# State mixer's jobs ahead of the attention's at each point, and its within-chunk products in column halves

## The chip, the cores and the metric

One Trainium2 chip, one of its cores. The metric is the device time of one execution in microseconds. Five engines work side by side, each through its own list in order: TensorE (PE; its weight loads are shown as PEld), VectorE (DVE), ScalarE (ACT), GpSimd (POOL) and SyncE (SP), which issues most transfers. Semaphores order them against each other.

## What is computed

One layer of a diffusion backbone over 512 latent tokens (width 1024) and 256 context tokens: a norm with modulation, one input projection, four token mixers side by side, a gated merge, an output projection, and a mixture of experts. Two of the mixers matter here. Cut to what matters:

```python
def _window_attention(q, k, v, k_ctx, v_ctx, sink):      # 8 heads, 4 blocks of 128 queries
    s_loc = einsum("bqkgd,bjkd->bkgqj", qn, kn) * scale  # window of 3 blocks, masked
    s_ctx = einsum("bqkgd,bckd->bkgqc", qn, k_ctx) * scale
    probs = softmax(concatenate([s_loc, s_ctx, sink_col], -1))
    return p_loc @ vn + p_ctx @ v_ctx

def _ssd(x, dt, a, bm, cm, init, with_output):           # 8 heads, chunks of 128, forward and backward
    a_cs = cumsum(dt * a); xd = x * dt[..., None]
    chunk_states = einsum("bcqhn,bcqhp->bchpn", bc * decay_to_end[..., None], xd)
    final, prev = scan(step, init, (chunk_states, chunk_decay))
    lmat = exp(where(tri, a_cs[i] - a_cs[j], -inf))
    scores = einsum("bcihn,bcjhn->bcijh", cc, bc) * lmat
    y_diag = einsum("bcijh,bcjhp->bcihp", scores, xd)    # the within-chunk products
    y_off = einsum("bcihn,bchpn->bcihp", cc, prev) * exp(a_cs)[..., None]

def _merge(h, branches, w_gate, b_gate, w_branch, w_o):
    gates = sigmoid(h @ w_gate + b_gate)
    return sum(gates * einsum("blnw,nwd->blnd", branches, w_branch)) @ w_o
```

## The kernel before

The order of work is written out by hand. `timeline()` (lines 70 to 149) returns one list of steps, and every engine's program walks through that same list, each issuing its own instructions of a step. So a step's place in the list is its place in the queue of PE, DVE, ACT and POOL at once, and what an engine waits for in one step holds up all steps behind it on that engine. `bank_plan` (line 196) gives each step its bank of PSUM; `claim` (line 578) makes PE wait until the former user of the bank was read.

The stretch of interest is the merge. For each of the four branches in `MIX_ORDER` (3 short convolution, 2 Fourier, 0 attention, 1 state mixer) and each of 8 column tiles d there is a step `gate` (24 products of 128x512) and a step `proj` (12 of them). Behind each of them `side()` (line 125) is called twice; each call is a point, counted by `point`. On odd points it gives out the next step of the attention, on even points the next entry of the state mixer's list `ssm`.

The attention's steps work on a pair of heads or on one: `S` makes scores (DVE scales, masks and takes the maximum, lines 1798 to 1821; ACT takes the exponentials), `T` transposes the probabilities on PE (line 1045; on DVE a `T` step of odd number normalises two later heads, line 1822; ACT copies the result to PT), `O` multiplies with the values (line 1054; DVE copies the result to attT, line 1830). A block of queries with five key blocks takes the fifth one's scores in the bank that `O` uses.

The state mixer's steps, for direction d, chunk c and group g:

- `st`: the state of a chunk. POOL makes xdd (line 2190), PE multiplies (line 976), DVE combines it with the former state (lines 1831 to 1847: tmpS, then prevS). All ten use one bank.
- `G`: products of C and B for a chunk, masked on DVE to Gm (line 1848).
- `seg`: the decay matrix of a chunk and group. POOL fetches the decay rows with a broadcasting transfer to Am once the former E is made (line 2202), subtracts and clips in 4 instructions for each direction (line 2206), and for g = 0 also makes xd (line 2211), for which it waits for `y` of the former chunk. ACT takes the exponential to E (line 1415) once the former `y` no longer reads E. DVE multiplies E by Gm (line 1861).
- `yoff`: products with the former states (line 995), read by DVE with a factor (line 1862).
- `y`: the within-chunk products (line 1008), 4 heads by 2 directions of 128x128 weights (E) over 64 columns (xd), accumulated; DVE adds all parts and multiplies by the gate z (line 1869).
- `ynorm`, `ytr`: the norm and the transposes at the end.

Each product of 32-bit operands appears in the trace as two passes.

Two more names. Each weight tile of the stream is split in two parts that together keep its precision: ring_hi on ACT, ring_lo on DVE, also at steps of the list (`split_at`). At the first `proj` of each branch the branch itself is split in bhi (ACT) and blo (DVE), lines 1426 to 1434 and 1893 to 1898. The experts' first weights are fetched by SP once the last merge is done (line 652).

The list of the state mixer before, for one chunk c, has six entries, that is three pairs of gate and proj:

```python
scans += [[G(c,0), G(c,1), seg(c,0,0), seg(c,0,1)], [], [yoff(c,0), yoff(c,1)],
          [y(c,0)], [seg(c,1,0), seg(c,1,1)], [y(c,1)]]
```

Of the kernel before, what the change touches and what calls it, by code (L numbers as in the profile page):

```python
# [26 lines left out]
P = 128  # L27
# [5 lines left out]
HD = 64  # L33
# [11 lines left out]
HALF = BLK // 2  # L45
# [24 lines left out]
def timeline():  # L70

    t = [("mr", 0), ("ssq",), ("mr", 2), ("mod", 0), ("xa", 0), ("mr", 1), ("xa", 1), ("mr", 3), ("modb",), ("csq",), ("xbc", 0)]
    t += [("v", c) for c in range(NCH)]
    t += [("ssqc",), ("xbc", 1), ("fu", 0), ("xbcc", 0), ("vc",), ("xbcc", 1), ("dt",)]
    macc = 0

    def tile(*jobs):


        nonlocal t, macc  # L80
        t += [*jobs, ("macc", macc)]
        if macc > 4 and macc % 4 == 1:
            t += [("mod", macc // 4)]
        macc += 1

    for m in range(2, 6):
        tile(("xbc", m), ("xbcc", m))
    tile(("k",), ("kc",))
    for m in range(1, 4):
        tile(*([("rope", 0)] if m == 2 else []), ("fu", m), *([("rot", 0)] if m == 1 else []))  # L90
    t += [("dec",)]
    for m in range(4):
        tile(*([("rope", m - 1)] if m > 1 else []), ("q", m), *([("rot", m)] if m else [("decr",)]))
    for m in range(4):
        tile(*([("rope", 3)] if m == 0 else []), ("cg", m), *([("rot", 4)] if m == 0 else []))
        tile(*([("rope", 4)] if m == 0 else []), ("sx", m))
        if m < 3:
            tile()
        tile(("bg", m))
    for i in range(4):  # L100
        tile(("zk", i))
    t += [("macc", 31)] + [("z", c) for c in range(NCH)]
    t += [("xtr", c) for c in (4, 5, 0, 1, 2, 3)] + [("btr", 0), ("btr", 1), ("mod", 8)]

    att_step = 0

    def attention():

        nonlocal att_step
        h, att_step = att_step, att_step + 1  # L110
        even = h % 2 == 0
        return ([("O", h // 2 - 2)] * (even and h >= 4) + [("T", h - 2)] * (2 <= h < 34) + [("S", h // 2)] * (even and h < 32))

    t += attention() + [("V", 0), ("V", 1), ("F", 0), ("V", 2), ("F", 1), ("V", 3)] + attention()
    t += [("F", 2), ("F", 3)] + attention() + attention()

    ssm = [[("st", d, k)] for k in range(5) for d in range(2)]
    scans = [[], [], []]
    for c in range(NCH):
        scans += [[("G", c, 0), ("G", c, 1), ("seg", c, 0, 0), ("seg", c, 0, 1)], [], [("yoff", c, 0), ("yoff", c, 1)],  # L120
                  [("y", c, 0)], [("seg", c, 1, 0), ("seg", c, 1, 1)], [("y", c, 1)]]
    scans += [[("ynorm",)], []] + [[("ytr", c), ("ytr", c + 1)] for c in (0, 2)]
    point = 0

    def side():

        nonlocal point
        point += 1
        if point % 2 == 1 and att_step < 35:
            return attention()  # L130
        if ssm and point % 2 == 0:
            return ssm.pop(0)
        return []

    for i, n in enumerate(MIX_ORDER):
        if i == 1:
            ssm += scans
        if i == 3:
            t += [x for jobs in ssm for x in jobs]
            ssm = []  # L140
        for d in range(8):
            t += [("gate", n, d)] + side() + side() + [("proj", n, d)] + side() + side()
    for d in range(8):
        if d == KD - 1:
            t += [("rtk", 5), ("rtf",)]
        t += [("wo", d)] + ([("sw",)] if d == 4 else []) + ([("rtk", d - 2)] if 1 < d < KD - 1 else [])
    t += [("rtk", 6), ("ssq2",), ("rtk", 7), ("rt",)] + [("h2tr", c) for c in range(NCH)] + [("g2",), ("cnt",), ("pick", 0), ("bexp",), ("pick", 1),
                                                                   ("up0",), ("tab",)]
    return t
# [158 lines left out]
def build(nc, xT, ctxT, adaw, stream, consts, cossin, dft, cols, rows, wv, wrt, umap, wa, wb, w2, h2d, ybuf, csd, gfin, out):  # L308
# [29 lines left out]
    E = at("E", 65536, [P, 2, S])  # L338
# [32 lines left out]
    xd = at("xd", 173248, [P, 2, S])  # L371
    H = at("H", 177344, [P, KD, S])
    CT = at("CT", 193728, [P, C_N])
    o = 193728 + C_N * 4
# [92 lines left out]
    def bk(b, n=1):  # L467

        return psum[:, b:b + n, :].rearrange("p b n -> p (b n)")
# [234 lines left out]
    def _(pe):  # L704
        def mm(out, lhsT, rhs, start, stop):
            return nc.tensor.matmul(out, lhsT, rhs, start=start, stop=stop)  # L706
# [112 lines left out]
        for s in steps:  # L819
            k0 = s[0]  # L820
            if k0 in ("ssq", "ssqc"):
                b = claim(pe, s)
                pe.wait_ge(sum_ready, 1 if k0 == "ssq" else 2)
                if k0 == "ssq":
                    ins = mm(bk(b), one_t[:, :], sq[:, 0, :], True, True)
                else:
                    for i in range(2):
                        ins = mm(bk(b)[:, 0:SC], one_t[:, :], sq[:, KD, i * SC:i * SC + SC], i == 0, i == 1)
                ins.then_inc(full[b], 1)
            elif k0 == "mod" and s[1]:  # L830

                b = claim(pe, s)
                pe.wait_ge(macc_ready, 4 * s[1])
                for j in range(4):
                    ins = mm(bk(b)[:, 2 * j:2 * j + 2], macc[s[1] % 2][:, j * P:j * P + P], CT[:, C_ONE:C_ONE + 2], True, True)
                ins.then_inc(full[b], 1)
            elif k0 == "mr":

                b = claim(pe, s)
# [11 lines left out]
                for k in range(KD):  # L851
                    q = k % 4 * 32
                    ins = mm(bk(b)[q:q + 32, :], silp[:, k, :], ada[u][:, k * S:k * S + S], k < 4, k >= 4)
# [30 lines left out]
            elif s == ("xbc", 0):  # L884
# [8 lines left out]
                for k in range(4, KD):  # L893
                    ins = lo_block(k)
# [11 lines left out]
            elif k0 == "vc":  # L906
                b = claim(pe, s)
                pe.wait_ge(h_ready, 2 * KD)
                for i in range(NCC):
                    for k in range(KD):  # L910
                        ins = mm(bk(b)[:, i * VD:i * VD + VD], hcx[:, k, i * P:i * P + P], WV[:, k, :], k == 0, k == KD - 1)
                ins.then_inc(full[b], 1)
            elif k0 == "zk":
# [3 lines left out]
                for c in range(NCH):  # L917
                    b = claim(pe, ("z", c)) if s[1] == 0 else plan[("z", c)][0]
                    for kk in range(2):
                        k = 2 * s[1] + kk  # L920
                        ins = three(bk(b), Hhi[:, k, c * P:c * P + P], Hlo[:, k, c * P:c * P + P], hi[:, kk * S:kk * S + S],
                                    lo[:, kk * S:kk * S + S], k == 0, k == KD - 1)
# [6 lines left out]
            elif k0 == "dec":  # L929
                b = claim(pe, s)  # L930
                pe.wait_ge(dta_ready, 1)
                sums = bk(b)[:, 0:288].rearrange("p (c n) -> p c n", n=48)
                for col, (m, r0, r1) in zip((0, 8, 16, 24, 32), ((C_LE, 0, 8), (C_GE, 8, 16), (C_GT, 0, 8),
                                                                 (C_LT, 8, 16), (C_ONE, 0, 16))):
                    ins = mm(sums[:, :, col:col + r1 - r0], CT[:, m:m + P], dta[:, :, r0:r1], True, True)
                ins.then_inc(full[b], 1)
            elif k0 == "decr":
                b = claim(pe, s)
                pe.wait_ge(csr_ready, 1)
                nc.tensor.transpose(bk(b)[0:NCH * 16, 0:P], csr[:, :, :].rearrange("p c n -> p (c n)"), ID).then_inc(full[b], 1)  # L940
            elif k0 == "xtr":
                b = claim(pe, s)
                pe.wait_ge(xbc_ready, 6)
                o = chunk_cols(s[1])
                for m in range(4):
                    ins = nc.tensor.transpose(bk(b)[:, m * P:m * P + P], xbcT[:, m, o:o + P], ID)
                ins.then_inc(full[b], 1)
            elif k0 == "btr":
                b = claim(pe, s)
                for i in range(3):  # L950
                    o = chunk_cols(3 * s[1] + i)
                    ins = nc.tensor.transpose(bk(b)[:, i * P:i * P + P], xbcT[:, 4, o:o + P], ID)
                ins.then_inc(full[b], 1)
            elif k0 == "V":
                b = claim(pe, s)
# [6 lines left out]
                for c in range(NCH):  # L962
                    ins = mm(bk(b, 2)[:, c * 256:c * 256 + 256], uT[:, ft, c * P:c * P + P],
                             CT[:, C_BD:C_BD + 256], True, True)
                ins.then_inc(full[b], 1)
            elif k0 == "F":
                b = claim(pe, s)
# [8 lines left out]
            elif k0 == "st":  # L976
                d, k = s[1:]
                b = claim(pe, s)
# [29 lines left out]
            elif k0 == "y":  # L1008
# [3 lines left out]
                pe.wait_ge(xd_ready, 2 * (c + 1))  # L1012
                for h in range(4):
                    for d in range(2):
                        ins = mm(bk(b)[:, h * HD:h * HD + HD], E[:, d, h * P:h * P + P],
                                 xd[:, d, (g * 4 + h) * HD:(g * 4 + h) * HD + HD], d == 0, d == 1)
                ins.then_inc(full[b], 1)
            elif k0 == "ytr":
                b = claim(pe, s)
# [1405 lines left out]
```

## Time and profile before

| what | value |
|---|---|
| time, median of 3 runs | 1158.52 us (1158.37 to 1160.19) |
| the profiled execution's own time | 1160.84 us |
| its span, first to last instruction | 1159.0 us |
| PE busy | 1094.2 us, 94% of the span |
| DVE, ACT, POOL busy | 562.2, 317.3, 178.7 us |
| mean granted clock of TensorE | 0.986 of full speed |
| chain that ended last | PE 71%, DMA 14%, DVE 8%, ACT 3% |

The profile is of one execution. Times in it count from the first instruction. A group of instructions is told by its line, its engine and what it writes and reads; line 706 is the helper through which all products of PE go, line 1547 that of most of DVE's, line 1244 that of ACT's. Behind an instruction or group stands the time for which its engine sat idle before it, and what ended that. The merge lies between 280 and 647 us.

### The profile page before, as it was taken

Reading aid. Unit: us, or ns where it says so; the run is one execution under the profiler, and the core shown is the slowest. Engines: PE = TensorE matmul, PEld = TensorE weight load, DVE = VectorE, ACT = ScalarE, POOL = GpSimd, SP = SyncE. Lnnn points to the kernel's source line nnn. Section 1 sums busy time; section 2 is a strip of 40 time slices with the busy share of each in tenths; the row PEclk is TensorE's granted clock in tenths of the full one; section 3 lists DMA queues with packets and bytes.
Section 4 is the critical chain, followed back from the end, with each engine's and each line's share of the span. In section 5 each row is a group of like instructions: output and inputs, shape, how many; then the busy total and the mean of one; then the engine's idle time right before and its main releaser. Section 6 shows DMA issues by size and latency. Waiting matters only on the chain.

```text
span 1159.0 us, 16301 instructions
## 1 busy us (share of the span) xinstructions
PE 1094.2 (94%) x5691; PEld 701.2 (61%) x5691; DVE 562.2 (49%) x1011; ACT 317.3 (27%) x539; POOL 178.7 (15%) x255
## 2 busy tenths in 40 slices
PE   6999999989999999999999998999999899978985
PEld 4788888878667777878888777333333233322333
DVE  5776787744676778757564547221112111111214
ACT  4543322244344554333433242100000000000003
POOL 0000010000110223256000100122212112211220
PEclk9999999999999999999999998999999999999998
DMA  9523855720111122214122488999999999999975
GB/s 373 202 95 117 299 170 202 254 92 19 56 55 56 73 74 74 90 74 146 56 109 93 178 369 331 406 379 424 424 423 425 425 424 426 426 427 425 426 313 224
DMA packets 41982, 279.68 MB, mean 241 GB/s; under 512 B 7803, under 2 KB 8187, under 8 KB 30017
## 3 DMA queue, kind: packets, MB, share of 16 engines
q1 hardware_dynamic: 34496, 265.07, 56.9%
q0 software_dynamic: 7424, 13.80, 3.5%
q8 instruction: 38, 0.62, 0.2%
q14 instruction: 24, 0.19, 0.0%
HBM read 274.23 MB, written 13.40 MB: 248 GB/s over the span
## 4 chain that ended last, share of the span: by engine, by line
PE 71%; DMA 14%; DVE 8%; ACT 3%; issue 2%; POOL 1%; SPq 0%; DVEq 0%; ACTq 0%; POOLq 0%
PE psum L706 68%; DMA ering<-in_wb 8%; DMA ering<-in_wa 2%; DMA ada<-in_adaw 2%; DVE ring_lo L1547 1%; PE psum L722 1%; DVE amx L1818 1%; ACT ring_hi L1244 1%; DVE sc L1807 1%; PE psum L1052 1%; DMA xr<-token_rows,tabt 1%; PE psum L746 1%; DMA Hx<-in_xT 1%; POOL Am L2206 1%; PE psum L1136 0%
## 5 line engine op out<-in xcount | busy, mean ns | idle before, releaser
L706 PE MATMUL psum<-ering,xs 128*64 128x512 f32 x1056 | 240.2, 606 | 17.4 <-DMA ering<-in_wb 9.4
L706 PE MATMUL psum<-Hhi,ring_hi 128*128 128x512 f32 x472 | 188.0, 398 | 0.1
L706 PE MATMUL psum<-Hlo,ring_hi 128*128 128x512 f32 x472 | 185.3, 393 | 0.2 <-DVE Hlo L1547 0.2
L706 PE MATMUL psum<-Hhi,ring_lo 128*128 128x512 f32 x472 | 183.1, 390 | 0.0
L706 PEld LDWEIGHTS psum<-ering,xs 128*64 128x64 f32 x1056 | 74.0, 139 | 162.1 <-issue 137.5
L1547 DVE TENSOR_TENSOR ring_lo<-ring,ring_hi 128x1024 fp32r<-128x1024 f32 x87 | 107.9, 1240 | 107.8 <-ACT ring_hi L1244 106.7
L1547 DVE TENSOR_TENSOR sg<-sg,psum 128x256 f32<-128x256 f32 x66 | 27.8, 421 | 238.3 <-ACT sg L1244 237.2
L706 PE MATMUL psum<-ering,at 128*64 128x512 f32 x528 | 119.5, 597 | 2.8 <-ACT at L1244 1.6
L1244 ACT ACTIVATE ring_hi<-ring 128x1024 fp32r<-128x1024 f32 x87 | 92.2, 1060 | 74.8 <-DMA ring<-in_stream 41.8
L706 PEld LDWEIGHTS psum<-Hhi,ring_hi 128*128 128x128 f32 x472 | 88.7, 188 | 22.7 <-issue 3.2
L706 PEld LDWEIGHTS psum<-Hhi,ring_lo 128*128 128x128 f32 x472 | 88.5, 188 | 19.7
L706 PEld LDWEIGHTS psum<-Hlo,ring_hi 128*128 128x128 f32 x472 | 88.7, 188 | 18.1 <-DVE Hlo L1547 0.5
L1244 ACT ACTIVATE sg<-psum 128x256 f32<-128x256 f32 x33 | 12.7, 384 | 250.4 <-PE psum L706 250.4
L706 PEld LDWEIGHTS psum<-ering,at 128*64 128x64 f32 x528 | 35.9, 136 | 67.1 <-issue 66.4
L1547 DVE TENSOR_TENSOR ysb<-psum,G 128x512 f32<-128x512 f32 x33 | 22.8, 691 | 94.9 <-PE psum L706 80.6
L2206 POOL TENSOR_SCALAR Am<-Am,csr 128x128 f32<-128x128 f32 x64 | 53.7, 852 | 33.9 <-DMA Am<-decay_rows 33.2
L706 PE MATMUL psum<-bhi,ring_hi 128*128 128x512 f32 x128 | 53.2, 416 | 2.4 <-DVE blo L1547 2.4
L706 PE MATMUL psum<-blo,ring_hi 128*128 128x512 f32 x128 | 51.0, 398 | 0.0
L706 PE MATMUL psum<-bhi,ring_lo 128*128 128x512 f32 x128 | 50.9, 398 | 0.0
L1244 ACT ACTIVATE gth<-psum,half 128x512 f32<-128x512 f32 x32 | 22.0, 689 | 102.4 <-PE psum L706 100.0
L1244 ACT ACTIVATE at<-psum 128x256 f32<-128x256 f32 x33 | 12.7, 384 | 124.0 <-PE psum L746 124.0
L2234 POOL DMA_INDIRECT expert_rows<-ysb,idx x33 | 33.7, 1020 | 84.0 <-DVE ysb L1547 83.1
(355 smaller groups left out, 1447.0 us busy)
## 6 DMA issues: line engine op xcount, KB each, us to landing
ering<-in_w SPq DMA_DIRECT2D x28, 2048.0 KB, 21.6
ering<-in_wb SPq DMA_DIRECT2D x28, 2048.0 KB, 27.8
ering<-in_wa SPq DMA_DIRECT2D x28, 2048.0 KB, 22.8
ring<-in_stream SPq DMA_DIRECT2D x87, 512.0 KB, 4.2
ada_ring<-in_stream SPq DMA_DIRECT2D x32, 512.0 KB, 3.6
ada<-in_adaw SPq DMA_DIRECT2D x4, 2048.0 KB, 10.7
Am<-decay_rows POOLq DMA_DIRECT2D x8, 512.0 KB, 4.6
gat<-expert_rows SPq DMA_DIRECT2D x4, 1024.0 KB, 8.1
```

Source lines behind the costliest of these rows:

```text
L706: return nc.tensor.matmul(out, lhsT, rhs, start=start, stop=stop)
L722: ins = nc.tensor.transpose(XT[h][:, q * P:q * P + P], xr[h][:, q * P:q * P + P], ID)
L746: ins = nc.tensor.transpose(AT[h][:, q * P:q * P + P], sg[h][:, q * P:q * P + P], ID)
L1052: ins = nc.tensor.transpose(bk(b, 2)[:, i * P:i * P + P], sc[:, h % 3, i * P:i * P + P], ID)
L1244: return nc.scalar.activation(out, in_, f, **kw)
L1547: return V_.tensor_tensor(out, a, b, op)
L1807: ins = V_.scalar_tensor_tensor(sc[:, h % 3, 0:S], bk(3 + g), HD ** -0.5, CT[:, C_MASK + mo:C_MASK + mo + S], ALU.mult, ALU.add)
L1818: link(V_.tensor_reduce(amx[:, h, 0:1], sc[:, h % 3, 0:W], AX.X, ALU.max))
L2206: G_.tensor_scalar(Am[:, d, h * P:h * P + P], Am[:, d, h * P:h * P + P], csr[:, c, x:x + 1], 0.0, ALU.subtract, ALU.min).then_inc(*t(am_re ...
L2234: G_.indirect_dma_start(out=row_half, in_=rows_[:, :], in_offset=None, out_offset=bass.IndirectOffsetOnAxis(ap=idx[:, 2 + h:3 + h], axis=0 ...
```

## The change

Attention and state mixer change places: the state mixer's steps come on odd points, the attention's on even ones, so at each gate and proj the state mixer's step stands first in the list. In each chunk `seg(c,1)` moves one entry forward, to stand right behind `y(c,0)`; with `seg(c,0)` in the first entry the segments are now three entries apart. `y(c,1)` keeps its entry. And `y`'s products are issued in halves of 64 weight columns, which write to the lower and the upper 64 partitions of the bank.

```diff
@@ timeline
         scans += [[("G", c, 0), ("G", c, 1), ("seg", c, 0, 0), ("seg", c, 0, 1)], [], [("yoff", c, 0), ("yoff", c, 1)],
-                  [("y", c, 0)], [("seg", c, 1, 0), ("seg", c, 1, 1)], [("y", c, 1)]]
+                  [("y", c, 0), ("seg", c, 1, 0), ("seg", c, 1, 1)], [], [("y", c, 1)]]
@@ side
-        if point % 2 == 1 and att_step < 35:
+        if point % 2 == 0 and att_step < 35:
             return attention()
-        if ssm and point % 2 == 0:
+        if ssm and point % 2 == 1:
             return ssm.pop(0)
@@ PE, step y
                 for h in range(4):
                     for d in range(2):
-                        ins = mm(bk(b)[:, h * HD:h * HD + HD], E[:, d, h * P:h * P + P],
-                                 xd[:, d, (g * 4 + h) * HD:(g * 4 + h) * HD + HD], d == 0, d == 1)
+                        for i in range(2):
+                            o = h * P + i * HALF
+                            ins = mm(bk(b)[i * HALF:i * HALF + HALF, h * HD:h * HD + HD], E[:, d, o:o + HALF],
+                                     xd[:, d, (g * 4 + h) * HD:(g * 4 + h) * HD + HD], d == 0, d == 1)
```

## Rows read from the trace of the kernel before

**Rows 1.** Busy time by stretch: window, length, busy and count by engine, clock, DMA share, GB/s

```profile
252.00:645.00 393.00, 379.65 (x2199) 304.32 (x2200) 254.32 (x475) 160.81 (x266) 79.35 (x89) 0.99 0.21 73
...
800.00:1000.00 200.00, 194.84 (x904) 65.90 (x906) 36.09 (x68) 12.58 (x33) 41.65 (x68) 0.99 1.01 425
```

**Rows 2.** Waits of PE, 252 to 660: who for whom, us in total, times, longest

```profile
PE psum L706 <- DVE prevS L1547: 3.9, 4, 1.2
PE psum L706 <- DVE blo L1547: 2.4, 1, 2.4
PE psum L706 <- DVE attT L1830: 2.4, 4, 0.8
PE psum L706 <- DVE yt L1547: 1.7, 2, 1.5
PE psum L706 <- DVE tmpS L1841: 1.6, 1, 1.6
```

**Rows 3.** Timeline of DVE and PE at the second st: start, length, instruction [idle before]

```profile
290.05 0.69 DVE L1807 SCALAR_TENSOR_TENSOR sc<-psum,CT 128x512 f32<-128x512 f32 x1
...
293.44 0.42 DVE L1841 COPY tmpS<-psum 128x256 f32<-128x256 f32 x1
...
293.92 0.65 PE L706 MATMUL psum<-xdd,btm 128*64 128x256 f32 x4 [1.63 <-DVE tmpS L1841]
```

**Rows 4.** Timeline of PE: first product of a gate, and of the proj behind it

```profile
589.01 0.40 PE L706 MATMUL psum<-Hhi,ring_hi 128*128 128x512 f32 x1
...
594.53 0.39 PE L706 MATMUL psum<-bhi,ring_hi 128*128 128x512 f32 x1
```

**Rows 5.** Timeline of DVE, 434 to 442: the reads of yoff

```profile
437.36 0.69 DVE L1547 TENSOR_TENSOR ytmp<-psum,dec 128x512 f32<-128x512 f32 x1
438.09 0.69 DVE L1547 TENSOR_TENSOR yt<-psum,dec 128x512 f32<-128x512 f32 x1
```

**Rows 6.** Timeline of ACT, POOL and DVE, 484 to 512: two segments, then the branch split

```profile
487.20 1.30 ACT L1244 ACTIVATE E<-Am 128x512 f32<-128x512 f32 x2
...
489.03 0.78 POOL L2202 DMA_DIRECT2D Am<-decay_rows  x1 [14.64 <-ACT E L1244]
...
502.43 0.63 ACT L1244 ACTIVATE E<-Am 128x512 f32<-128x512 f32 x1 [4.20 <-POOL Am L2206]
...
505.52 2.50 DVE L1547 TENSOR_TENSOR blo<-attT,bhi 128x512 fp32r<-128x512 f32 x4
```

**Rows 7.** Busy time by stretch: the first proj of the attention branch

```profile
506.35:510.72 4.37, 4.37 (x12) 3.20 (x12) 2.89 (x4) 1.77 (x3) 2.17 (x2) 0.65 0.34 138
```

**Rows 8.** Groups by line, 252 to 660, POOL: busy us, mean ns | idle before

```profile
L2206 POOL TENSOR_SCALAR Am<-Am,csr 128x128 f32<-128x128 f32 x64 | 53.7, 852 | 33.9 <-DMA Am<-decay_rows 33.2
...
L2211 POOL TENSOR_TENSOR xd<-xs,dtv 128x512 f32<-128x512 f32 x8 | 9.7, 1212 | 0.6 <-PE psum L706 0.6
```

**Rows 9.** The page's DMA issues: count, KB each, us to landing

```profile
Am<-decay_rows POOLq DMA_DIRECT2D x8, 512.0 KB, 4.6
```

**Rows 10.** Timeline of PE: products of O, y, the modulation and an expert

```profile
438.84 1.31 PE L706 MATMUL psum<-PT,vt 128*64 128x128 f32 x20 [1.46 <-DVE yt L1547]
...
441.76 2.00 PE L706 MATMUL psum<-xd,E 128*128 128x64 f32 x16
...
252.06 1.05 PE L706 MATMUL psum<-CT,macc 128*128 128x2 f32 x8 [0.64 <-ACT btm L1244]
...
980.04 7.09 PE L706 MATMUL psum<-ering,xs 128*64 128x512 f32 x32
```

**Rows 11.** Groups by line, 252 to 660, PE and PEld: y's products, the two loads

```profile
L706 PE MATMUL psum<-xd,E 128*128 128x64 f32 x128 | 15.5, 274 | 0.0
...
L706 PEld LDWEIGHTS psum<-PT,vt 128*64 128x64 f32 x288 | 15.4, 136 | 7.2 <-issue 5.0 <-DVE yt L1547 1.9 <-DVE Gm L1547 0.4
L706 PEld LDWEIGHTS psum<-xd,E 128*128 128x128 f32 x128 | 15.2, 192 | 0.7 <-issue 0.2
```

**Rows 12.** The tile Am: duration of its instructions, ns least, median, most

```profile
L2206 POOL TENSOR_SCALAR Am<-Am,csr x64: 702/716/1667, 398.3 to 547.3; 128x128 f32<-128x128 f32 x64
```

## The prediction

> **What bounds the kernel now.** The profiled execution took 1160.84 us, 1.84 us more than its span of 1159.0; the median of the three runs is 1158.52. I sum the change against the profiled execution and then set it off from the median, which lies 2.3 us lower. First the table by stretch: in the stretch of the gate and projection products, 252 to 645 us, TensorE (PE) is busy for 379.65 of 393 us, VectorE (DVE) for 254, ScalarE (ACT) for 161 and GpSimd (POOL) for 79 [rows 1]. So PE sets the pace, and two things can be won: its 13 us of idle time, and instructions of its own. The experts behind it run on weight transfers (DMA share 1.01 from 800 to 1000 us [rows 1]), and by the code the first of these waits for the last merge. So what the stretch loses in length, the end should lose too.
>
> Second, the waits of PE [rows 2]: 3.9 + 1.6 us behind the state combinations on DVE (prevS, tmpS), 1.7 behind `yoff` and `y` work (yt), 2.4 behind the split of the attention branch (blo), 2.4 behind the copy of attention rows (attT). All are head-of-line waits: DVE works its list in order, and the wanted instruction stands behind attention work.
>
> **Part 1: `st` ahead of the attention.** PE reached the second `st` when its bank was still unread: the read, tmpS at 293.44, stood on DVE behind the two softmax heads that began at 290.05; PE went on at 293.92 after 1.63 us idle [rows 3]. After the change `st` leaves PE and DVE before O, T and S, so its bank is read while PE does attention and a projection (2.8 us, half of the gate's 5.5 [rows 4]). I take all of 3.9 + 1.6 = 5.5 us away (bounds: 3 to 5.5). What is late next: the projection's `st` is read at most 1 us after the projection's own DVE pair, and the next `st` is a whole gate (5.5 us) later. POOL's product for the next `st` waits only for the former `st` on PE, which comes earlier too. On the other side, DVE's copy of O now stands behind `st`, and the fifth key block of S waits for that copy. Three of the four attT waits lie in places without `st` and stay; the one with `st` can grow by the two DVE instructions of a combination less the `st` products that now fill PE: 0.85 us (an estimate, twice the 0.42 of tmpS [rows 3]) less 0.55, so +0.3.
>
> **Part 2: `yoff` and `y` ahead.** At 437 PE waited 1.46 us for yoff's reads, which stood behind two softmax normalisations; the reads take 0.69 each from 437.36 [rows 5]. Placed ahead they end sooner by the two normalisations, more than the wait: the 1.7 us of yt waits go to nothing (bounds 0.3 to 1.7). New waits stand in their place. On PE `y` waits for the masked E and for xd, and O, T and S are now queued behind it; its segment is two or three points back, a gate at least, so I count no wait. On ACT the second segment's exponentials wait for `y`, and the copy of T is queued behind them; the next O needs it a gate later. On DVE `y` and the masking of E (`seg`) stand ahead of O and S: DVE begins S's heads some 3 us later in four places (an estimate). The next transposes of probabilities stand a projection and a gate away, and by my count 1.4 us remain at the tightest (an estimate). I set +1.5 us for new waits over the stretch (bounds 0 to 6): nothing in the trace shows this order, and the remaining slack is nearest to nothing lost.
>
> **Part 3: `seg` three points apart.** Before, the second segment's exponentials (E at 487.20) waited on ACT for their place behind two transposes and a projection, POOL's next transfer waited 14.64 us for them (489.03), and the last exponential began at 502.43 and ended at 503.06; behind it in line stood the copies and splits of which blo, from 505.52, is the one that PE's first projection of the attention branch needs [rows 6]; PE began it at 506.35 [rows 7]. After the change the segment stands right behind `y(c,0)`, which follows the gate: six us earlier. What is late next is `y(1,1)`, for which POOL waits before its product xd. It stands ahead of O now; behind its end PE still has O (1.1), a projection (2.8), two small G (0.4, an estimate) and a gate (5.5), 9.8 us. In that time POOL makes xd (1.2) and four Am of 0.85 [rows 8], ACT an exponential (0.63), and the rest takes 506.35 − 503.06 = 3.3 as before: 8.5. It leaves 1.3 us, so the 2.4 go (bounds 1 to 2.4). With them goes a second loss: right behind this gap the granted clock was 0.65 over 506.35 to 510.72 [rows 7], that is in part at the lower of its two levels, 1.2 GHz, and the projection took 4.37 us instead of 2.8: 1.5 us. Sum 3.9.
>
> A transfer of decay rows, a POOL queue entry, moves with the segment; 4.6 us to landing [rows 9] at a DMA share of 0.21 [rows 1] is covered. Moved past it on that queue is nothing but `st` products, long done.
>
> **Part 4: within-chunk products in column halves.** Eight `y`, each 16 passes of 128 weight columns over 64 moving columns. From the timeline: (2.00 − 0.27) / 15 = 0.115 us a pass, and 8 passes over only 2 moving columns take (1.05 − 0.25) / 7 = 0.114 [rows 10] (the last pass taken off, 0.27 [rows 11]; 0.25 for the narrow one is an estimate). So a pass costs what loading 128 columns costs, whatever moves. The change makes 32 passes of 64 columns, in two column groups. Loading 64 columns takes 192 − 136 = 0.056 us less than 128 [rows 11], that is half. And two column groups work at once: O's 20 passes of this shape over 128 columns take 1.31 us, (1.31 − 0.27) / 9.5 = 0.109 for a pair (0.27 for the last pass [rows 11]; half a pair more for the first load), and 32 over 512 take 7.09, at most 0.443 a pair [rows 10]. Four times the columns, four times the time: no floor shows down to 0.109, and the loading hides. At 64 columns a pair should take 0.056, and 16 pairs with a first load and a change of array shape 0.9 + 0.16 = 1.05 us against 1.8. I take 0.75 × 8 = 6.0 us (bounds: 0, if 0.109 is the least for a pair, to 7). No semaphore is added.
>
> The Trainium skill speaks against this part. "TensorE: Matmul & The Clock Gate", Part 3, What overlaps, says that loading weights overlaps running products only where the row groups differ; column halves use the same rows. By that rule load and product follow each other and the sum would lose the 6 us. The trace disagrees as far as O reaches: its pairs at 0.109 leave no room for a load of 0.056 beside 128 columns [rows 10], and O's groups share their rows.
>
> **Sum.** −5.5 + 0.3 − 1.7 − 3.9 − 6.0 + 1.5 = −15.3 us. Profiled 1160.84 − 15.3 = 1145.5; from the median 1158.52 − 15.3 = **1143.2 us**.
>
> **Rivals.**
> *The halves give nothing* (a pair has a floor at O's 0.109: 16 × 0.109 + 0.1 = 1.8 us, as now). For it: no row has a shorter pair. Against it: the proportion from 128 to 512 columns. Time 1158.5 − 9.3 = 1149.2. The skill's rule above would give the same.
> *DVE becomes the queue that PE waits for*: with `y` and `seg` ahead of S, the probabilities come late in the chunks that still have attention. DVE is at 65% of the stretch [rows 1], so it needs a bad order, not too much work. If DVE is 3 us later than I count in the four places, and 1.4 of each is slack, PE waits 4 × 1.6 = 6.4 us more: 1143.2 + 6.4 = 1149.6, and with the halves giving nothing 1155.6.
> *The waits only move*: PE meets the same unread banks at the gate's `st`. Then 5.5 us come back: 1148.7. Against it: a gate of 5.5 us stands between.
> *Slower: POOL's decay chain becomes the bound.* Per chunk it has two transfers of 4.6 [rows 9], 16 Am of 0.85, two xd of 1.2 [rows 8], and about 3.5 of issue and exponentials: 28.7 us. PE's chunk without attention is 3 × (5.5 + 2.8) + 1.5 + 2 × 1.05 = 28.5 (estimate), so there is no slack beyond what chunk edges give. If Am rose to the 1.67 us of its slowest one [rows 12], a chunk would take 41.8; chunks 2 and 3 and the wait for the normalisation would cost PE 2 × 13 = 26 us against 15 won, 1169. It decides from a mean Am of about 1.5. For it: Am goes from 0.70 to 1.67 in one trace, so something does stop it. The skill's "GPSIMD Engine Reference", 1. Specifications, names the memory interface shared with VectorE as such a thing. Against it: the mean is 0.85 at the present load, DVE's work is not more, and `y` stands two points behind its segment.
> *It doesn't do what it says*: the instructions are issued in the order of the list, so only the halves could fail this, and that is the first rival.
>
> **How the numbers follow.** Forecast as summed 0.62; halves give nothing 0.17; DVE late, or waits that move, 0.12; POOL chain 0.05; mixtures that end near no change 0.04. What a measurement of this kernel can tell from no change is about 0.2%, 2.3 us. Faster by more 0.87; the same 0.06; slower 0.07 (the chain and half of the mixtures). The range: downwards all bounds at their best, −5.5 − 1.7 − 3.9 − 7 = −18.1, 1140.4, and 1.4 for how the executions differ: 1139. Upwards the halves at 0 and 3 us of waits beyond what I set, 1152.2: 1152.
>
> **What would show it.** In the trace after: no PE waits for tmpS, prevS, yt and blo, and attT waits of 2.4 to 2.7 us; the granted clock at 1.00 at the first projection of the attention branch; `y` at 32 passes of 128*64 within 1.1 us, where 1.8 would show the floor; POOL's wait for E between the segments shorter than 14 us and the Am mean near 0.85. The forecast is wrong if PE's idle time in the stretch is still above 9 us, if new waits for probabilities (T behind DVE's sc) appear, or if the length won in the stretch is lost again between the last merge and the experts.

## The result and the profile after

The changed kernel takes 1152.93 us (median, 1151.3 to 1153.95), the kernel before 1158.52 beside it: a ratio of 0.9946, 95% interval 0.9931 to 0.996. It is faster, by 5.6 us and not by the 15.3 forecast, and 0.9 us above the range. The profiled executions differ by 1160.84 − 1152.93 = 7.9 us. The whole difference lies in the merge. From the first product of its first gate to the first product of the output projection behind it, PE took 647.20 − 279.88 = 367.3 us before:

```profile
279.88 0.47 PE L706 MATMUL psum<-Hhi,ring_hi 128*128 128x512 f32 x1
...
647.20 0.39 PE L706 MATMUL psum<-mhi,ring_hi 128*128 128x512 f32 x1
```

And now:

```profile
279.76 0.48 PE L706 MATMUL psum<-Hhi,ring_hi 128*128 128x512 f32 x1
...
639.26 0.39 PE L706 MATMUL psum<-mhi,ring_hi 128*128 128x512 f32 x1
```

that is 359.5, so −7.8; what comes behind it to the end of the span takes 511.8 us in both. I call this the length of the merge below. It is read from the same two products in each trace, and it leaves out the stretches ahead (278.3 to 280.9 us over all traces) and behind (510.2 to 513.2). But it is the length in one execution of each kernel, with the clock that this execution happened to be granted; the whole times are of 5 to 17 executions.

The waits of PE from 252 to 660 us (who for whom, us in total, times, longest) answer to [rows 2]:

```profile
PE psum L706 <- DVE attT L1832: 4.6, 5, 1.9
PE psum L706 <- DVE Gm L1549: 2.1, 1, 2.1
PE psum L1054 <- DVE sc L1589: 1.4, 1, 1.4
...
PE psum L706 <- DVE tmpS L1843: 0.9, 1, 0.9
...
PE psum L706 <- DVE ring_lo L1549: 0.3, 1, 0.3
PE psum L706 <- DVE blo L1549: 0.2, 1, 0.2
```

yt and prevS are gone, blo and tmpS nearly so. Gm and sc are new, and attT has grown from 2.4 to 4.6. Within the merge PE waited 12.05 us before (the five rows of [rows 2]) and waits 9.45 now. By stretch (window, length, busy and count of PE, PEld, DVE, ACT, POOL, clock, DMA share, GB/s), against [rows 1] and [rows 7]:

```profile
252.00:645.00 393.00, 381.68 (x2357) 303.34 (x2357) 260.35 (x482) 163.93 (x268) 81.37 (x92) 0.99 0.23 77
...
462.00:470.30 8.30, 7.18 (x34) 5.58 (x34) 6.38 (x15) 2.12 (x5) 6.79 (x8) 0.61 0.01 4
501.20:504.20 3.00, 2.98 (x14) 2.18 (x14) 2.96 (x4) 1.67 (x2) 3.00 (x3) 1.00 0.56 175
```

The first projection of the attention branch, at 501, now runs at full clock. But from 462 the granted clock is 0.61, right behind the new waits. What they cost and where they come from is one story on three engines. The timeline (start, length, instruction, [idle before]) of DVE, ACT and PE around 456 us:

```profile
454.39 0.21 DVE L1821 TENSOR_SCALAR amx<-amx,RW 128x1 f32<-128x1 f32 x1
454.70 0.72 ACT L1246 ACTIVATE sc<-sc,amx 128x512 f32<-128x512 f32 x1 [0.69 <-DVE amx L1821]
...
455.73 1.06 ACT L1246 ACTIVATE ring_hi<-ring 128x1024 fp32r<-128x1024 f32 x1
...
456.89 1.23 DVE L1549 TENSOR_TENSOR ring_lo<-ring,ring_hi 128x1024 fp32r<-128x1024 f32 x1 [2.29 <-ACT ring_hi L1246]
...
458.15 0.69 DVE L1907 SCALAR_TENSOR_TENSOR mtmp<-gth,psum 128x512 f32<-128x512 f32 x1
...
459.60 1.01 DVE L1549 TENSOR_TENSOR Gm<-psum,CT 128x128 f32<-128x128 f32 x4
...
460.64 1.42 DVE L1549 TENSOR_TENSOR E<-E,Gm 128x512 f32<-128x512 f32 x2
...
460.66 1.09 PE L706 MATMUL psum<-PT,vt 128*64 128x128 f32 x16 [2.11 <-DVE Gm L1549]
...
462.49 0.49 DVE L1589 TENSOR_SCALAR sc<-sc,amx 128x512 f32<-128x512 f32 x1
...
463.12 1.09 PE L1054 MATMUL psum<-CT,sc 128*128 128x128 f32 x4 [1.36 <-DVE sc L1589]
```

DVE ends the last maximum of S at 454.60. Next in its list is ring_lo, the second half of a weight split for a gate two column tiles on. It needs ring_hi, which on ACT stands behind the exponentials of the same S, and these wait for the maximum that DVE has just made. So DVE stands still for 2.29 us, although mtmp and Gm behind ring_lo could run: what they read is long made. The masking of E could not, as its E comes from ACT, behind the same ring_hi. O finds its bank (the one of G) unread for 2.11 us, T finds its probabilities not normalised for 1.36 (DVE's normalisation, sc at 462.49, comes behind Gm and E), and the clock falls. It is no isolated place. The waits of DVE in the merge up to the last `y`, first of the kernel before, then of the changed one:

```profile
DVE ring_lo L1547 <- ACT ring_hi L1244: 40.7, 22, 5.7
```

```profile
DVE ring_lo L1549 <- ACT ring_hi L1246: 40.7, 20, 6.2
```

That row was in the trace of before, and it is not among the rows that the prediction rests on.

### The profile page after: what moved, and what is told of

The parts are those of the page before. It is cut to its first block, busy times and chain, and to the rows that moved or that the text cites. A ratio compares the mean times of both kernels' runs of the same rounds, so it can differ in the third digit from the quotient of the medians.

```text
span 1151.1 us, 16557 instructions
## 1 busy us (share of the span) xinstructions
PE 1086.0 (94%) x5819; PEld 693.4 (60%) x5819; DVE 563.5 (49%) x1011; ACT 317.2 (28%) x539; POOL 178.4 (16%) x255
## 4 chain that ended last, share of the span: by engine, by line
PE 70%; DMA 15%; DVE 9%; ACT 3%; issue 2%; SPq 0%; DVEq 0%; POOL 0%; ACTq 0%; POOLq 0%
PE psum L706 66%; DMA ering<-in_wb 8%; DMA ering<-in_wa 2%; DMA ada<-in_adaw 2%; DVE ring_lo L1549 2%; PE psum L1054 1%; ACT ring_hi L1246 1%; PE psum L722 1%; DMA xr<-token_rows,tabt 1%; PE psum L746 1%; DVE amx L1820 1%; DMA WV<-in_wv 1%; DVE sc L1809 1%; DMA gat<-expert_rows 0%; ACT gth L1246 0%
## 5 line engine op out<-in xcount | busy, mean ns | idle before, releaser
L706 PE MATMUL psum<-ering,xs 128*64 128x512 f32 x1056 | 237.0, 599 | 19.1 <-DMA ering<-in_wb 10.8
L706 PEld LDWEIGHTS psum<-Hhi,ring_hi 128*128 128x128 f32 x472 | 88.7, 188 | 20.4 <-issue 1.1
```

## The experiments

Two theories of where the missing 9.7 us (15.3 − 5.6, in the medians) went. **Queue**: the change does what the sum says, but DVE's splits that wait for ACT stand in its list between the moved steps, so the time saved on PE is met by new waits of PE for DVE. **Small parts**: one or more terms of the sum (halves, order, segment) are simply worth less than forecast. The second can be seen by doing one part alone, the first by moving the splits. All ratios are to runs of the kernel before on the same chip.

**The halves alone.** Only the hunk of `y` in the diff, with the order of before.

```diff
...
+                        for i in range(2):
+                            o = h * P + i * HALF
+                            ins = mm(bk(b)[i * HALF:i * HALF + HALF, ...], E[:, d, o:o + HALF], ...)
```

> The kernel before with the products of y in column halves and nothing else. If each y falls from 1.7 to 1.8 us to about 1.0 and PE alone sets the pace, eight of them give 5.7 us: 1152.8 from 1158.5. If the freed time is taken back by the waits that are already there (the split of the attention branch behind POOL's decay chain, 2.4 us, would grow), 1155 or more. If both halves of the change were independent, this and the order alone would add up to the whole.

Measured: 1157.36, ratio 0.9979 (0.9968 to 0.9991); length of the merge 362.1. The eight `y` fall as in the changed kernel (8.6 us in all, start to start, for 13.9), but the median shows less than half of it. The reason that the expectation gave for this is not what the trace shows: the wait for blo did not grow (2.1 for 2.4), and PE's waits in the merge are 12.6 us for 12.05. The traced execution was the fastest of its twelve.

**The order alone.** The changed kernel without the hunk of `y`.

```diff
-                        for i in range(2):
...
+                        ins = mm(bk(b)[:, h * HD:h * HD + HD], E[:, d, h * P:h * P + P], ...)
```

> The changed kernel with y at full width: the order and the segments as changed, the column halves undone. If the halves are worth the 5.7 us that the trace shows for y, this is 1158.6, no gain at all from the order, its old waits (8.0 us and a slow projection) replaced by new ones (4.9 us and a slow gate). If the halves only shift waits, it lies near 1153.

Measured: 1153.48, ratio 0.9941 (0.9925 to 0.9957); merge 362.9, that is −4.5 where the order's terms sum to −9.3. The first expectation, 1158.6 and no gain at all, missed by 5 us; the time is that of the other, by which the halves only shift waits. In the whole times the halves on top of this order indeed show nothing clear of the noise (ratios 0.9941 and 0.9946); in the traces they shorten the merge by 3.4, as 2.0 of their 5.3 us turn into waits of PE (7.43 us in the merge here, 9.45 in the changed kernel). Its waits of PE, 252 to 660 us:

```profile
PE psum L706 <- DVE attT L1830: 4.5, 5, 1.9
...
PE psum L1052 <- DVE sc L1587: 1.4, 1, 1.4
...
PE psum L706 <- DVE tmpS L1841: 0.9, 1, 0.9
PE psum L706 <- DVE Gm L1547: 0.5, 1, 0.5
```

So the new waits come with the order (two stretches of low clock too, see the end); with the shorter `y` the one for Gm is 2.1 instead of 0.5.

**State steps ahead only while `st` lasts** (point 32), then as before.

```diff
+        swap = point <= 32
-        if point % 2 == 1 and att_step < 35:
+        if point % 2 == (0 if swap else 1) and att_step < 35:
-        if ssm and point % 2 == 0:
+        if ssm and point % 2 == (1 if swap else 0):
```

> The kernel before with the state steps alone ahead of the attention (the first branch), the scans behind it as before, y at full width. The five waits of 5.5 us should go, 0.9 come at the second of the gate's st, and the wait for the copy of attention rows grow by 1.1: 3.5 us, 1155.0. If the order of st does nothing but move waits, 1158.

Measured: 1153.86, ratio 0.9955 (0.9941 to 0.997); merge 360.4. Of the `st` waits 0.9 is left (tmpS), attT is 3.5, yt stays at 1.7, and blo falls to 1.4 though the segment has not moved. This part alone gives nearly all that the whole change gives, so the rest of it wins and loses about the same.

**The segment alone** moved behind `y(c,0)`, with all else as before.

```diff
-                  [("y", c, 0)], [("seg", c, 1, 0), ("seg", c, 1, 1)], [("y", c, 1)]]
+                  [("y", c, 0), ("seg", c, 1, 0), ("seg", c, 1, 1)], [], [("y", c, 1)]]
```

> The kernel before with the second segment moved to stand right behind y(c,0) and nothing else (attention still ahead, full-width y). Prediction's Part 3: the wait for blo (2.4 us) goes and the projection behind it runs at full clock (1.5 us): 3.9 us below before, 1155. Rival: with y and state behind the attention as before, the chain from the segment to blo is as long as it was and the wait stays: no change from before, 1158.5 to 1159.5.

Measured: 1157.11, ratio 0.9981 (0.997 to 0.9992), between the two expectations; merge 364.0, −3.3. The wait for blo fell from 2.4 to 0.4 and no low clock follows it (timeline of PE):

```profile
504.92 0.47 PE L706 MATMUL psum<-bhi,ring_hi 128*128 128x512 f32 x1 [0.40 <-DVE blo L1547]
```

**Late splits.** The changed kernel; on DVE a ring_lo that is listed at a `proj` is made at the next gate. Nothing is left out, only DVE's order changes.

```diff
+        late = []
...
+            if k0 in ("gate", "wo") or s in split_at and k0 != "proj":
+                for i in late:
+                    split_lo(i)
+                late = []
+            if k0 == "proj":
+                late += split_at.get(s, [])
+            else:
                 for i in split_at.get(s, []):
                     split_lo(i)
```

> The changed kernel; on DVE alone the low part of a weight tile that falls due at a projection (every second one) is made at the next gate instead, ahead of nothing that PE needs within 12 us. Theory: the new waits of PE (0.9 at an st, 1.1 more at the fifth key block, 2.1 at O and 1.4 at T in the second chunk, and the half clock behind them, about 2.5) come from DVE standing idle 2.3 us there for the high part, which on ACT is queued behind the exponentials of the scores that DVE has just made. Then they go and the time falls by 5 to 8 us, to 1145 to 1148. Rival: DVE has simply too much work in those places; then the waits stay and the time is 1152 to 1153.

Measured: 1145.17, ratio 0.9874 (0.9856 to 0.9892); merge 352.4. The waits for Gm, sc and tmpS are gone, and no low clock is left in the merge. What is left of PE's waits there, beside 0.3 and 0.2 for ring_lo and blo:

```profile
PE psum L706 <- DVE attT L1840: 4.0, 5, 1.2
...
PE psum L706 <- ACT PT L1246: 0.4, 1, 0.4
```

DVE goes on standing still for ring_hi, 30.5 us in 12 places instead of 40.7 in 20. So the idle time as such is not what costs; it costs where work that PE wants soon stands behind it.

**All splits late**: those listed at O, `st` and `y` too, to just ahead of the next projection or gate.

```diff
+        late, merging = [], False
...
+            if k0 in ("gate", "proj", "wo"):
+                for i in late:
+                    split_lo(i)
+                late, merging = [], True
+            if merging and k0 not in ("gate", "wo"):
+                late += split_at.get(s, [])
+            else:
                 for i in split_at.get(s, []):
                     split_lo(i)
```

> The changed kernel, with all of DVE's ring_lo splits of the merge that do not belong to the step at hand put behind the work that TensorE waits for: those that stood ahead of a projection are made at the next gate, those that stood ahead of O, st or y are made just before the next projection or gate. Queue theory (DVE stood still for ACT's ring_hi with wanted work behind it): the attT waits (1.24 and three of .54) and the wait of G(2,0) (1.12) go too, 3 to 4 us below the 1145.2 of late_split, so 1141 to 1142, with no wait of TensorE above 0.6 us between 280 and 636 us. Rival (what is left is DVE's and ACT's own pace of work): nothing more is won, 1145.

Measured: 1139.3, ratio 0.9827 (0.9811 to 0.9843), beside 1152.59 for the changed kernel on the same chip; merge 346.9. This beats both kernels, and the expectation by 2 us. PE has no wait in the merge any more, and DVE hardly one for ring_hi; the same place as above, all in its order:

```profile
DVE ring_lo L1549 <- ACT ring_hi L1246: 0.8, 1, 0.8
```

```profile
449.30 0.21 DVE L1829 TENSOR_SCALAR amx<-amx,RW 128x1 f32<-128x1 f32 x1
449.55 0.69 DVE L1915 SCALAR_TENSOR_TENSOR mtmp<-gth,psum 128x512 f32<-128x512 f32 x1
...
450.64 1.06 ACT L1246 ACTIVATE ring_hi<-ring 128x1024 fp32r<-128x1024 f32 x1
451.00 1.01 DVE L1549 TENSOR_TENSOR Gm<-psum,CT 128x128 f32<-128x128 f32 x4
...
454.87 1.09 PE L706 MATMUL psum<-PT,vt 128*64 128x128 f32 x16
...
455.78 1.22 DVE L1549 TENSOR_TENSOR ring_lo<-ring,ring_hi 128x1024 fp32r<-128x1024 f32 x1
```

DVE goes straight on from the maximum to mtmp and Gm; ring_lo follows at 455.78, when ring_hi has long been made. O starts without a wait.

> The changed kernel as it is, on the same chip as the three others, so that they can be set against it: 1152.9 to 1154.

Measured for the changed kernel once more: 1152.59, ratio 0.9945 (0.9931 to 0.996); merge 360.0, and the waits are the same to 0.02 us each.

**Late splits in the order of before**: the two hunks above put on the kernel before, full-width `y`.

> The kernel before, its order and its full-width y unchanged, with only the late splits of late_split. If the late splits are worth their gain with the new order alone, the waits for tmpS and prevS (5.5 us), which stand behind softmax heads and not behind a split, stay: 1155 to 1157 (before 1158.5 to 1159.7), won from yt 1.5 and part of blo 2.4. If the splits were the whole of the 14.5 us that late_split won: about 1150 with the y of before.

Measured: 1157.09, ratio 0.9985 (0.997 to 0.9999); the `st` waits stay at 3.9 + 1.6, yt falls from 1.7 to 0.3, and the first projection of the attention branch now waits 1.6 us for bhi on ACT in blo's place.

> The kernel before, its order and its full-width y unchanged, with the late splits of late_both. With late_both_full_y (new order, late splits: 1147.5), order_alone (new order, splits as before: 1153.5) and before (1158.9) it makes a square. If the order is worth 9 to 10 us once the splits are out of the way, against 5 to 6 with them in it: about 1157, with the st waits (5.5 us) as they were, since these stand behind softmax heads and not behind a split. If the splits alone bring the gain and the order little: 1149 to 1150, without st waits.

Measured: 1155.28, ratio 0.9971 (0.9957 to 0.9986); merge 361.4. DVE waits 1.2 us in all for ring_hi, and PE still waits:

```profile
PE psum L706 <- DVE prevS L1547: 3.3, 4, 1.1
PE psum L706 <- DVE blo L1547: 1.7, 1, 1.7
PE psum L706 <- DVE tmpS L1849: 1.6, 1, 1.6
```

So the splits alone don't bring the gain: with the softmax heads ahead, `st` waits whatever the splits do.

**Full-width `y` with late splits**, in both forms: the hunk of `y` taken back, as in the order alone.

> late_split with the within-chunk products as before (16 passes of 128 weight columns). If the 5.7 us that TensorE saves in y are worth their full size once it does not wait for DVE: 1145.2 + 5.7 = 1150.9. If a shorter y only makes TensorE arrive earlier at the same waits: 1146 to 1147, with waits behind the shorter y in late_split that are missing here.

> late_both with the within-chunk products as before (16 passes of 128 weight columns). late_both leaves TensorE no wait above 0.1 us in this stretch, so the 5.7 us of shorter y should come back whole but for what stands beside y: late_split's gates that end at a y were 0.09 to 0.12 us longer than those of late_split_full_y (5.69 against 5.60, 5.61 against 5.49) and its projections behind a y 0.03, some 0.9 us over eight: 1139.3 + 4.8 = 1144.1. If a shorter y is worth no more than the 3.2 us between late_split and late_split_full_y: 1142.5. If nothing: 1139.3.

Measured: 1148.36, ratio 0.9915 (0.9899 to 0.9931), merge 356.2; and 1147.52, ratio 0.9889 (0.9872 to 0.9906), merge 352.2. The second, like all splits late, has no wait of PE in the merge, so its 352.2 − 346.9 = 5.3 us is the clean price of full-width `y`, near the 4.8 expected. (The medians differ by 8.2, so the time expected, 1144.1, was missed by 3.4; in the profiled executions 1.5 lies behind the merge, where no `y` is.) In the first form the time lies between its two expectations, and the merge shows 3.8: there PE, earlier by the shorter `y`, waits 4.83 us in the merge against 4.03.

**The segment back at its old place, all splits late**, the rest as changed.

```diff
-                  [("y", c, 0), ("seg", c, 1, 0), ("seg", c, 1, 1)], [], [("y", c, 1)]]
+                  [("y", c, 0)], [("seg", c, 1, 0), ("seg", c, 1, 1)], [("y", c, 1)]]
```

> late_both with the second segment one attention point later, where it stood before (two points ahead of its y). Prediction's Part 3: GpSimd's transfer waits for the segment's exponentials again (14 us instead of about 10) and the first projection of the attention branch for blo, 2 to 2.4 us, with 1.5 us of half clock behind it in some executions: 1141.5 to 1143. Rival: blo stood late because of DVE's and ACT's queues of splits, and with these moved the segment's place is worth nothing: 1139.3.

Measured: 1139.9, ratio 0.9836 (0.9818 to 0.9853); merge 347.3, with one wait for blo of 0.4. The expectation of 2 us failed: with the state steps ahead and the splits late, the segment's place hardly matters (0.4 us of merge).

The lengths of the merge together, all with full-width `y`:

| | splits as before | all splits late | difference |
|---|---|---|---|
| order of before | 367.3 | 361.4 | −5.9 |
| new order, segment moved | 362.9 | 352.2 | −10.7 |
| difference | −4.5 | −9.3 | |

With the splits out of the way the new order is worth 9.3 us in these traces, with them in it half. Part of that contrast is the clock: the order alone was traced with two stretches at the low clock, the kernel before with one, the two kernels with late splits with none. The whole times give the order 6.8 us with the splits in it (ratio 0.9941) and 9.5 without (0.9889 against 0.9971), and by their intervals these two are not surely apart. PE's waits in the merge, which repeat from one execution to the next (9.45 and 9.49 us in the two traced executions of the changed kernel), fall from 12.05 to 7.43 with the splits in it, and from 7.13 to none without. So the order and the late splits help each other by about 2.5 us, and the rest of the contrast is not shown. That 9.3 is also the sum of the prediction's terms for the order is in part luck: this sum holds 1.5 us for a slow clock that the kernel with late splits in the old order did not have, and 1.5 the other way for new waits.

Of the two theories, the first holds: the new waits go when the splits move. Small parts were not the reason, since order and halves bring 9.3 and 5.3 us once the splits are out of the way.

## Why the prediction was wrong

**The failed step is in Part 2**: "+1.5 us for new waits (bounds 0 to 6)", with its count that "1.4 us remain at the tightest" on DVE and "nothing in the trace shows this order". The prediction gives the outcome of this count alone, and no wait of DVE for ring_hi stands in it or in the rows. It left out that DVE already stood still for ring_hi 40.7 us in the merge before, up to 5.7 at a time, and that the moved steps come to stand behind such an instruction. Busy shares hid it: 65% of the stretch looked like room, but in-order work behind an instruction that waits is no room. Four new waits came: 2.11 (Gm), 1.36 (sc), 0.26 (ring_lo) and 1.12 for the copy of attT ahead of `G(2,0)`, together 4.85 against 1.5. That is still inside the bounds 0 to 6; what lies in no bound is the low clock behind the waits, below. Gm and sc are gone with the first form of late splits, the other two with the second. The rival "DVE becomes the queue that PE waits for" had the mechanism, but its price rested on the same count, and it had a share of 0.12.

The same cause spoiled a part of **Part 1**. Of the 5.5 us 4.6 went, inside the bounds; 0.89 stayed at tmpS, behind ring_lo at 296.76, which had waited 2.29. The attT wait with `st` grew by 1.13 instead of 0.3. DVE's timeline and PE's show why:

```profile
327.70 1.23 DVE L1549 TENSOR_TENSOR ring_lo<-ring,ring_hi 128x1024 fp32r<-128x1024 f32 x1
328.96 0.42 DVE L1549 TENSOR_TENSOR ytmp<-prevS,cds 128x256 f32<-128x256 f32 x1
329.42 0.42 DVE L1549 TENSOR_TENSOR prevS<-ytmp,psum 128x256 f32<-128x256 f32 x1
329.87 0.29 DVE L1832 COPY attT<-psum 128x128 f32<-128x128 f32 x1
...
330.21 0.49 PE L706 MATMUL psum<-kT,qT 64*128 64x128 f32 x4 [1.89 <-DVE attT L1832]
```

The two instructions of `st` that I counted are there (0.42 each), and a 1.23 us split ahead of them, which I did not count as a thing that the copy is now behind. DVE was late there already, as it had stood still 2.40 us for another ring_hi up to 322.01. With all splits late this wait is 0.

**The clock** was counted as a gain of 1.5 only. The gain came: the projection takes 2.97 instead of 4.37. But behind the new waits T, S and the projection from 463.12 took 1.02, 2.01 and 4.06 us from start to start; with all splits late the same steps take 0.59, 1.09 and 2.99. That is 2.4 lost, in no term of the sum.

**Part 3** was right in size where it was meant: blo from 2.40 to 0.18, POOL's wait for E between the segments 10.52 instead of 14.64 [rows 6], Am at 835 ns instead of 852 [rows 8] (timeline and groups of POOL):

```profile
480.49 0.78 POOL L2204 DMA_DIRECT2D Am<-decay_rows  x1 [10.52 <-ACT E L1246]
```

```profile
L2208 POOL TENSOR_SCALAR Am<-Am,csr 128x128 f32<-128x128 f32 x64 | 52.6, 835 | 32.7 <-DMA Am<-decay_rows 31.9
```

It holds for the segment alone too in the traces (−3.3 against −3.9 forecast); the whole times show 2.2 (0.9 to 3.5). What the prediction did not see is that it is one of two cures: where the other is there, the move is worth 0.4.

**Part 4** was right. A `y` takes 0.98 us from start to start where the next product is O's, and 1.08 where it is a projection; before it was 1.81 and 1.70, so 5.7 us in eight, against 6.0. In the clean pair (both with all splits late) it is 1.82 and 1.70, so 5.8, and the merge gets 5.3 of them. The half microsecond between lies at the edge: the first half-width pass starts later behind a gate. Timeline of PE with full-width `y`, then with halves (both with all splits late):

```profile
428.85 0.39 PE L706 MATMUL psum<-Hhi,ring_lo 128*128 128x512 f32 x1
429.08 1.89 PE L706 MATMUL psum<-xd,E 128*128 128x64 f32 x16
430.90 1.31 PE L706 MATMUL psum<-PT,vt 128*64 128x128 f32 x20
```

```profile
428.62 0.39 PE L706 MATMUL psum<-Hhi,ring_lo 128*128 128x512 f32 x1
428.94 1.15 PE L706 MATMUL psum<-xd,E 128*64 128x64 f32 x32
429.92 1.26 PE L706 MATMUL psum<-PT,vt 128*64 128x128 f32 x20
```

From the gate's last product to the first of `y` it is 0.23 us, then 0.32; the O behind gives 0.04 of that back (1.20 to the next step, not 1.24). The floor of 0.109 a pair does not exist: 0.98 / 16 is 0.061. By the estimates of the prediction a load of 64 columns takes 0.056, and the products of a pair take 0.055, half of O's 0.109. One behind the other that would be 0.11 a pair even if its two loads ran at once, so here loading runs beside the products. The Trainium skill has a rule ("TensorE: Matmul & The Clock Gate", Part 3, What overlaps) by which loading overlaps running products only where the row groups differ. The halves share their rows, so the 0.98 us of a `y` disagrees with it.

**The sum again**, measured terms against forecast: `st` −4.6 (−5.5), attT +1.1 (+0.3), yt −1.75 (−1.7), new waits +4.85 (+1.5), blo −2.2 (−2.4), clock at the first projection −1.4 (−1.5), clock behind the new waits +2.4 (0), halves −5.3 (−6.0): −6.9, where the merge shortened by 7.8. The 0.9 between stays open. Of the 7.5 us missing from the 15.3, waits of PE are 5.2 (−2.6 against −7.8), the clock 2.5 (+1.0 against −1.5) and the halves 0.7, less that 0.9. That the new waits and the low clock behind them have one cause is shown by the late splits: with them both are gone, and the change comes to 1139.3, a merge 20.4 us shorter than before. Of these the square gives 5.9 to the late splits and 9.3 to the order, and the clean pair 5.3 to the halves.

The medians miss 9.7 and the merge only 7.5. The other 2.2 lie in how the prediction went from its sum to its time: the sum was read in an execution of 1160.84, 2.3 us above the median of its kernel, and then set off from the median as if all of its losses were there too. The changed kernel's profiled execution is its median one. The 1.5 us of slow clock behind blo are a candidate for a loss that not every execution has, as the last section shows, but no run here shows how often it falls.

What the prediction named as signs came out: "new waits for probabilities (T behind DVE's sc)" and idle time above 9 us in the stretch (it is 393.00 − 381.68 = 11.3) are what its last part said would make it wrong. POOL's chain did not become the bound, and nothing was lost between the merge and the experts.

## What to carry to other kernels

Before moving work on an engine that looks a third idle, read that engine's own waits, not its busy share: an in-order engine that stands still for another engine has no room there for the work queued behind. A step that needs a partner engine's answer to what was just asked belongs behind the work that does not, above all when its own result is needed late; here that reorder was worth 13.3 us on the changed kernel, where the change itself was worth 5.6, and 3.3 on the kernel before. The change was worth about twice as much with it (14.5 us of merge for 7.8). A part whose gain depends on the queue is best priced twice, once with the queue as it is and once without.

## What the runs showed that was not expected

The clock fell behind some gaps and not behind others of the same length. Before, PE waited 2.4 us for blo and the clock then was 0.65 [rows 7]; with the halves alone it waited 2.12 in the same place, and it stayed at full speed (timeline of PE, and the stretch behind it):

```profile
502.85 0.47 PE L706 MATMUL psum<-bhi,ring_hi 128*128 128x512 f32 x1 [2.12 <-DVE blo L1549]
```

```profile
502.00:509.00 7.00, 6.15 (x29) 4.66 (x30) 6.49 (x9) 2.22 (x3) 4.40 (x5) 1.00 0.34 115
```

Likewise behind an attT wait of 1.9 us the clock was 0.72 from 329 to 335 us with the order alone, and 1.00 in the changed kernel and with the state steps ahead. A second traced execution of the changed kernel shows that it is not the kernel that decides. Behind the same wait of 1.89 us its clock fell:

```profile
331.00:337.00 6.00, 5.72 (x22) 3.80 (x23) 4.92 (x11) 2.21 (x6) 0.00 (x1) 0.72 0.00 0
```

So a gap of about 2 us is a risk of 1.5 to 2.5 us more, not a fixed price; what decides was not settled. It also blurs the single parts: the halves alone won 5.3 us of merge in the profiled execution and 2.4 in the median.
